# A shared 64 KB SBUF region for the PEER query weights, and twenty expert-table copies moved behind the last mixer block, in a streaming encoder step on one core

## The chip, the cores and the metric

One core of one Trainium2 chip. The metric is the device time of one execution in microseconds (us). The core's engines are named as the profile names them: PE (TensorE matmuls), PEld (its weight loads), DVE (VectorE), ACT (ScalarE), POOL (GpSimd) and SP (SyncE, which here only issues DMAs). POOL issues DMAs too: they run on the profile's queue q0. SP's run on q1.

## The reference

One layer over 1024 prompt frames (8 blocks of 128) and 8 x 16 sample frames (one block of 128): two mixers, then a PEER expert layer.

```python
h = rmsnorm(x, norm_mix)
qa, ka, va, qb, kb, vb, rg, ga, gb = project(h, w_in, b_gate)      # (1024, 5888)
oa = windowed attention(qa, ka, va)      # window 128, ALiBi, sinks
ob = retention(qb, kb, vb)               # per chunk, a state carried along
x += (sigmoid(ga) * (oa @ w_branch_a) + sigmoid(gb) * (ob @ w_branch_b)) @ w_out
h = rmsnorm(x, norm_ffn)
q = h @ w_q                              # (1024, 8 heads * 256)
s1, s2 = q1 @ sub_k1.T, q2 @ sub_k2.T    # 128 keys a side
idx, gate = best 16 of the 16 x 16 sums of the best 16 on each side, per head
u = expert_u[idx]; v = expert_v[idx]     # 128 rows of 1024 for each token
x += sum_k gate * gelu(h . u_k) * v_k
y = rmsnorm(x, norm_final)
```

Everything is float32. The outputs are y for both streams, the new key and value windows and the retention states.

## The kernel before

The 9 blocks of 128 tokens are block 0 (sample) and blocks 1 to 8 (prompt). The program is six `nc.Block` stages, one after another. At the end of each, the engines meet.

- **Stage A** (0 to 180 us): input projections of blocks 0 and 1.
- **Stage B** (to 346 us): the mixer of block 0.
- **Stage E** (to 458 us): the mixer of block 1. `prompt_buffers` and `score_buffers` give its tiles, among them the branch weights `wa` (16 KB a partition) and `wb` (32 KB), `wo` (32 KB), `zqk` (the part of z with queries and keys) and `alibi`. `pe_branches` multiplies by `wa` and `wb` and signals `ya`. `pe_output` then multiplies by `wo`. `store_rows` stores x and h2 when `x1` and `h2` are signalled.
- **Stage S** (to 1165 us): the expert search and experts of block 0, the search and the first 48 expert places of block 1, and the input projections of blocks 2 to 8 (line 1238). SP loads H, then with `load_search` the sub keys and all of `peer_w_q` (8 DMAs of 1 MB into `wq_s`), then the projections' inputs `xg` and the first two weight tiles `w`. PE waits for the query weights and runs `pe_keys` for two blocks, then the projections. POOL waits for the weights and for both tiles `w`, copies table parts, then gathers expert rows into `ring_s`.
- **Stage P** (to 1794 us): the mixers of blocks 2 to 8, one pass of a loop for each block; from pass 3 on a pass also ends the block before it (its branches, output, x and h2 stores). Between a block's steps `dve_point` puts expert groups of block 1: POOL gathers three rows of `peer_u` into `ru` (`pool_dots`) and three rows of `peer_v` into `rv` (`pool_values`), and DVE makes three dots (line 1472) and three accumulations (line 1489). Four such pairs of groups lie in a block, in a fixed order on DVE. The last, of dots, stands just ahead of `dve_residual` (line 446). After block 8 comes the stage's **tail**: block 8's own output, the last `rv` groups, and the query projection and search of block 2. For that, SP streams `peer_w_q` in 8 chunks of 1 MB through three buffers (`load_chunk`, line 1520). `qT`, the turned queries, lies over the first chunk buffer.
- **Last stage** (to the end): experts of blocks 2 to 8, 128 gathers for each block. One gather (line 2012) reads 8 KB per token, a row of u beside its row of v, from the interleaved table `uv_d` (128 MB, 128 parts). `load_search` loads `peer_w_q` once more (8 MB) on SP.

**The table.** `uv_d` is written by copies from DRAM to DRAM, one part being two DMAs of 512 KB. POOL issues parts 0 to 87 in stages A, B, E and S, at most two parts in flight (`pool_table`). SP issues parts 88 to 127 in stage P, eight in each of the passes 3 to 7 (`rest_of_table`, lines 244 and 245): two after the next block's `zqk` load, two when `prob` is signalled, two after the gates' load, two when the retention output `ro` is signalled. The first gather of the last stage waits for all of them.

**Order on SP's queue in the tail:** chunks 3 to 7, each when its buffer is free; then a wait for `x1` of block 8, the x store, a wait for `h2`, the h2 store, and the output of block 1.

## Time and profile before

| | us |
|---|---|
| median of 3 runs (4168.81, 4177.75, 4183.3) | 4177.75 |
| the profiled execution | 4131.7 |
| its span, first to last instruction | 4129.9 |

| engine | busy us | share of the span |
|---|---|---|
| PE | 3298.1 | 80% |
| PEld | 1643.4 | 40% |
| DVE | 2455.5 | 59% |
| ACT | 1088.2 | 26% |
| POOL | 1769.1 | 43% |

Read the DMA row first: the mean busy share of the 16 DMA engines in 40 slices of 103 us. Then come tables of stretches ("windows"), with each engine's busy time, PE's granted clock, the DMA share and the GB/s moved. A copy from DRAM to DRAM counts its bytes once.

### The profile page before, as it was taken

The page shows a single profiled execution, that of the slowest core. Times are in us where ns is not written, and L with a number is a line of the kernel's source. Part 1 is how long each engine was busy: PE and PEld are TensorE (multiplying, and loading weights), DVE is VectorE, ACT ScalarE, POOL GpSimd, SP SyncE. Part 2 cuts the span into 40 slices and gives each one's busy share as a digit, 9 for nine tenths or more (in the row PEclk, how much of TensorE's full clock was granted, in tenths as well). Part 3 has the DMA queues.
Part 4 walks back from the last instruction along what each step waited for, and adds up shares of the span by engine and source line. Part 5 has one row for each costly group of instructions (what it writes and reads, how often), then busy time and mean ns, then how long its engine had stood idle before and what let it go on. Part 6 is the DMA issues. An engine that isn't in the chain of part 4 may idle for free.

```text
span 4129.9 us, 32128 instructions
## 1 busy us (share of the span) xinstructions
PE 3298.1 (80%) x8957; PEld 1643.4 (40%) x8957; DVE 2455.5 (59%) x4977; ACT 1088.2 (26%) x2932; POOL 1769.1 (43%) x1588
## 2 busy tenths in 40 slices
PE   8775589999928878749779779878878977977776
PEld 5453256666524444324224323323323423422222
DVE  0122168998857677544864764674684585485454
ACT  2102011111113233213333333333333333323322
POOL 1020137787723333114444454444444444445554
PEclk9876799999958888969999999999999999999999
DMA  9898899999999998469999999999999999999998
GB/s 352 297 290 310 321 304 413 411 407 414 412 360 341 344 354 300 160 269 420 421 421 418 415 420 399 421 414 409 420 409 409 419 417 403 422 406 422 422 422 353
DMA packets 303586, 1563.05 MB, mean 378 GB/s; under 512 B 31280, under 2 KB 59184, under 8 KB 179888
## 3 DMA queue, kind: packets, MB, share of 16 engines
q0 software_dynamic: 228096, 1300.34, 78.7%
q1 hardware_dynamic: 60736, 239.86, 15.0%
q10 hardware_dynamic: 14592, 21.10, 1.4%
q8 instruction: 51, 0.84, 0.1%
q14 instruction: 111, 0.91, 0.1%
HBM read 1517.54 MB, written 179.04 MB: 411 GB/s over the span
## 4 chain that ended last, share of the span: by engine, by line
DMA 26%; PE 18%; issue 7%; DVE 4%; ACT 1%; POOL 1%; POOLq 0%; ACTq 0%; DVEq 0%
DMA ring<-uv_d,IXD_p 26%; PE ps L1807 14%; PE ps L1779 3%; DVE ring L1906 2%; ACT dg L1850 1%; DVE BV_p L979 1%; POOL ring L2012 1%; ACT GE_p L1844 0%; DVE BP_p L984 0%; DVE CA_p L989 0%; DVE VV_p L1332 0%; DVE CA_p L1397 0%; DVE DOT_p L1906 0%; DVE ACC L1887 0%; PE ps L1796 0%
## 5 line engine op out<-in xcount | busy, mean ns | idle before, releaser
L1807 PE MATMUL ps<-ring,dg 128*128 128x512 f32 x3584 | 1704.6, 614 | 474.3 <-ACT dg L1850 449.9
L2012 POOL DMA_INDIRECT ring<-uv_d,IXD_p x896 | 1082.3, 1208 | 1318.1 <-PE ps L1807 1068.0
L1906 DVE CUSTOM_DVE_ANT_0 ring<-ring,H 128x1024 f32<-128x1024 f32 x896 | 1094.2, 1223 | 907.3 <-DMA ring<-uv_d,IXD_p 886.6
L1807 PEld LDWEIGHTS ps<-ring,dg 128*128 128x128 f32 x3584 | 664.0, 194 | 1432.8 <-ACT dg L1850 714.3
L1238 PE MATMUL ps<-w,xg 128*128 128x368 f32 x1792 | 554.3, 472 | 2.0 <-ACT SC_s L936 2.0
L1844 ACT ACTIVATE GE_p<-DOT_p 128x2 f32<-128x2 f32 x448 | 91.1, 203 | 1502.6 <-DVE DOT_p L1906 1502.6
L1238 PEld LDWEIGHTS ps<-w,xg 128*128 128x128 f32 x1792 | 340.4, 190 | 215.5 <-ACT SC_s L936 2.2
L1850 ACT ACTIVATE dg<-gdi,GE_p 128x128 f32<-128x128 f32 x896 | 310.6, 393 | 46.6 <-ACT GE_p L1844 1.2
L1838 ACT ACTIVATE gdi<-ident,GD_p 128x128 f32<-128x128 f32 x896 | 303.1, 386 | 26.3 <-issue 19.9
L145 POOL DMA_DIRECT2D uv_d<-in_peer_u x88 | 45.6, 518 | 504.7 <-DMA uv_d<-in_peer_v 270.3
L1779 PE MATMUL ps<-wq,hT_p 128*128 128x512 f32 x384 | 197.9, 597 | 0.0
L1508 POOL DMA_INDIRECT rv<-in_peer_v,IXD x80 | 88.4, 1105 | 231.6 <-DVE AC L1489 215.2
L969 POOL DMA_INDIRECT ring_s<-in_peer_v,IXD_s x128 | 158.2, 1236 | 44.9 <-issue 38.4
L1101 DVE CUSTOM_DVE_ANT_0 ring_s<-ring_s,H_s 128x1024 f32<-128x1024 f32 x128 | 152.1, 1223 | 41.6 <-DMA ring_s<-in_peer_u,IXD_s 40.5
L969 POOL DMA_INDIRECT ring_s<-in_peer_u,IXD_s x128 | 152.6, 1192 | 47.3 <-issue 40.2
L226 PE MATMUL ps<-w,xg 128*128 128x368 f32 x512 | 161.4, 479 | 13.9 <-DMA w<-in_w_in 13.9
L1112 DVE SCALAR_TENSOR_TENSOR ACC_s<-ring_s,WG_s,ACC_s 128x1024 f32<-128x1024 f32 x126 | 157.1, 1290 | 13.3 <-DMA ring_s<-in_peer_v,IXD_s 12.9
L1267 ACT ACTIVATE zo<-ps,rstd 128x368 f32<-128x368 f32 x112 | 61.8, 566 | 373.4 <-PE ps L1238 371.9
L1516 POOL DMA_INDIRECT ru<-in_peer_u,IXD x80 | 82.1, 1027 | 151.7 <-DVE DOT L1472 117.1
L1472 DVE CUSTOM_DVE_ANT_0 ru<-ru,H 128x1024 f32<-128x1024 f32 x80 | 96.0, 1222 | 60.0 <-DMA ru<-in_peer_u,IXD 59.9
L226 PEld LDWEIGHTS ps<-w,xg 128*128 128x128 f32 x512 | 98.6, 193 | 76.0 <-issue 16.3
L1489 DVE SCALAR_TENSOR_TENSOR AC<-rv,WG,AC 128x1024 f32<-128x1024 f32 x80 | 102.7, 1284 | 40.8 <-DMA rv<-in_peer_v,IXD 36.1
(415 smaller groups left out, 2901.7 us busy)
## 6 DMA issues: line engine op xcount, KB each, us to landing
uv_d<-in_peer_u POOLq DMA_DIRECT2D x88, 512.0 KB, 5.4
uv_d<-in_peer_v POOLq DMA_DIRECT2D x88, 512.0 KB, 6.6
w<-in_w_in SPq DMA_DIRECT2D x8, 2944.0 KB, 15.1
w<-in_w_in SPq DMA_DIRECT2D x16, 1472.0 KB, 9.8
z_d<-zo ACTq DMA_DIRECT2D x16, 1288.0 KB, 18.8
uv_d<-in_peer_u SPq DMA_DIRECT2D x40, 512.0 KB, 9.6
uv_d<-in_peer_v SPq DMA_DIRECT2D x40, 512.0 KB, 11.3
ring<-uv_d,IXD_p POOLq DMA_INDIRECT x896, 11.2
```

Of the source, the lines that this page charges most:

```text
L226: mm = T.matmul(ps[:, m % AB, 0:WC], xg0[:, k, b * P:(b + 1) * P], w0[:, p % 2, n % 2, k, :], start=(k == 0), stop=(k == KT - 1))
L969: gather = g.indirect_dma_start(ring[:, n % RING, :], None, t["peer_u"] if kind == "u" else t["peer_v"], bass.IndirectOffsetOnAxis(ap=inde ...
L1101: V.tensor_tensor_reduce(out=row, in0=row, in1=H2[:], scale=1.0, scalar=0.0, op0=ALU.mult, op1=ALU.add, accum_out=DOT[:, k:k + 1]).then_in ...
L1112: V.scalar_tensor_tensor(ACC[:, k % 2], row, WG[:, k:k + 1], ACC[:, k % 2], ALU.mult, ALU.add).then_inc(d["freed"], 1)
L1238: mm = T.matmul(ps[:, n % AB, 0:WC], xg[:, k, b * P:(b + 1) * P], w[:, tile % 2, k, :], start=(k == 0), stop=(k == KT - 1))
L1489: V.scalar_tensor_tensor(AC1[:], row, WG1[:, k:k + 1], AC1[:], ALU.mult, ALU.add).then_inc(d["accz"], 1)
L1779: mm = T.matmul(bank(2 + n), hT[:, k, :], wq[:, k, n * 512:(n + 1) * 512], start=(k == 0), stop=(k == KT - 1))
L1807: mm = T.matmul(bank(6 + n), dg[:, k % DR, :], ring[:, k % RS, D + n * 512:D + (n + 1) * 512], start=(k == 0), stop=(k == NK - 1))
L1838: S.activation(gdi[:, k % GR, :], ident[:], ACT.Copy, scale=GD[:, k:k + 1]).then_inc(e["gdi"], 1)
L1850: S.activation(dg[:, k % DR, :], gdi[:, k % GR, :], ACT.Copy, scale=GE[:, k:k + 1]).then_inc(e["diag"], 1)
L1906: V.tensor_tensor_reduce(out=row, in0=row, in1=H2[:], scale=1.0, scalar=0.0, op0=ALU.mult, op1=ALU.add, accum_out=DOT[:, k:k + 1]).then_in ...
L2012: g.indirect_dma_start(ring[:, n % RS, :], None, uv_d, bass.IndirectOffsetOnAxis(ap=IXD[:, n:n + 1], axis=0)).then_inc(s_ring[n % RS], 16)
```

## The change

1. A region `rows64` of 64 KB a partition lives over stages E to the last. In stages E and P it holds `wa`, `wb`, `zqk` and `alibi` (and in P two of the three chunk buffers, over `zqk` and `alibi`). In stage S it holds the query weights `wq` and then the gather ring. In the last stage it holds `wq`.
2. In stage E, `load_queries` loads the 8 MB of query weights on SP's queue as soon as `ya` of block 1 is signalled, ahead of `store_rows`. Stage S no longer loads them.
3. In stage P, the passes 3 to 7 issue four table parts each in place of eight: two after the `zqk` load and two after the gates' load. SP's waits for `prob` and `ro` at that place go. The other 20 parts (108 to 127) are issued behind chunk 7 in the tail, with no wait of their own.
4. Chunks 6 and 7 stay where they land, as the last quarter of `wq`. For that `qT` moves from the first chunk buffer to `bg`. The other six chunks (6 MB) are loaded again in the tail when `ya` of block 8 is signalled, behind the 20 parts and ahead of the x store. The last stage loads no query weights.
5. `DOT1`, `GE1` and `WG1` shrink, and some tiles get other addresses.

```diff
-TABLE_A, TABLE_BS, TABLE_E, TABLE_S = 24, 46, 62, 88
+TABLE_A, TABLE_BS, TABLE_E, TABLE_S, TABLE_P = 24, 46, 62, 88, 108
...
+        def shared_rows():
+
+            return (rows64[:, 0:4 * D].rearrange("p (k n) -> p k n", k=4), rows64[:, 4 * D:FREE].rearrange("p (k n) -> p k n", k=KT),
+                    rows64[:, FREE:FREE + VB], rows64[:, FREE + VB:FREE + VB + HA * 2 * P].rearrange("p (h n) -> p h n", h=HA))
...
+        def load_queries(sp, blk, chunks):
+
+            sp.wait_ge(s["ya"], blk + 1)
+            for k in range(chunks):
+                sp.dma_start(wq[:, k], t["peer_w_q"][k * P:(k + 1) * P, :]).then_inc(s_cw, 16)
...
+        rows64 = sb(ctx, "rows64", [P, KT * PH * 256])
+        wq = rows64[:].rearrange("p (k n) -> p k n", k=KT)
+        FREE = 12 * D
...
                     load_branches(sp)
+                    load_queries(sp, 1, KT)
                     store_rows(sp, 1)
...
-        def load_search(sp):
+        def load_keys_tables(sp):
 
             sp.dma_start(kt[:, 0], t["sub_k1t"]).then_inc(s_cw, 16)
             sp.dma_start(kt[:, 1], t["sub_k2t"]).then_inc(s_cw, 16)
-            for k in range(KT):
-                sp.dma_start(wq[:, k], t["peer_w_q"][k * P:(k + 1) * P, :]).then_inc(s_cw, 16)
...
-            ring = sb(m, "ring_s", [P, RING, D])
+            ring = rows64[:].rearrange("p (r n) -> p r n", r=RING)
...
-            wqc = sb(b_, "wq_n", [P, 2, PH * 256])
+            wqc = rows64[:, FREE:].rearrange("p (j n) -> p j n", j=2)
...
-            qT = wqc[:, 0].rearrange("p (k n) -> p k n", n=P)
+            qT = bg[:].rearrange("p (k n) -> p k n", n=P)
...
-                        part = TABLE_S + 8 * (blk - 3)
+                        part = TABLE_S + 4 * (blk - 3)
                         if blk > 2:
-                            rest_of_table(sp, part, part + 2)
-                            sp.wait_ge(s["prob"], blk + 1)
-                            rest_of_table(sp, part + 2, part + 4)
+                            rest_of_table(sp, part, min(part + 2, TABLE_P))
...
-                            rest_of_table(sp, part + 4, part + 6)
-                            sp.wait_ge(s["ro"], blk + 1)
-                            rest_of_table(sp, part + 6, part + 8)
+                            rest_of_table(sp, part + 2, min(part + 4, TABLE_P))
...
                         load_chunk(sp, k)
+                    rest_of_table(sp, TABLE_P, NEXP // P)
+                    load_queries(sp, NB - 1, KT - 2)
                     sp.wait_ge(s["x1"], NB)
...
-            wq = sb(m, "wq", [P, KT, PH * 256])
...
-                            pe.wait_ge(s_cw, CW + 16 * (KT + 2))
+                            pe.wait_ge(s_cw, CW + 16 * KT)
...
-                    load_search(sp)
+                    load_keys_tables(sp)
```

## Rows read from the trace of the kernel before

**Rows 1.** The page: DMA busy share in tenths over 40 slices.

```profile
DMA  9898899999999998469999999999999999999998
```

**Rows 2.** Stretches: us, busy of PE, PEld, DVE, ACT, POOL, clock, DMA share, GB/s.

```profile
1250.00:1610.00 360.00, 290.92 (x993) 171.86 (x993) 255.89 (x403) 118.39 (x218) 128.74 (x118) 0.85 0.93 343
...
1725.00:1785.00 60.00, 33.41 (x84) 15.48 (x82) 56.88 (x212) 4.16 (x5) 0.00 (x0) 0.77 0.00 0
...
1860.00:2120.00 260.00, 218.59 (x523) 93.17 (x522) 177.21 (x420) 85.73 (x269) 123.19 (x104) 0.99 1.01 421
```

**Rows 3.** DMA issues, 1800 to 4100 us: queue, count, KB, us to landing.

```profile
wq<-in_peer_w_q SPq DMA_DIRECT2D x1, 1024.0 KB, 41.6
```

**Rows 4.** SP's timeline, first DMA of stage S: start, duration, line, tile, count.

```profile
458.45 0.34 SPq L1195 DMA_DIRECT2D H_s<-h_d  x1
```

**Rows 5.** DVE's timeline around `ya` in stage E.

```profile
423.79 1.22 DVE L438 TENSOR_TENSOR gates_e<-gates_e,ps 128x1024 f32<-128x1024 f32 x1 [24.37 <-PE ps L327]
```

**Rows 6.** PE's timeline: first instruction of stage S, in brackets its wait.

```profile
484.21 1.97 PE L907 MATMUL ps<-ident,H_s 128*128 128x128 f32 x8 [36.98 <-DMA wq_s<-in_peer_w_q]
```

**Rows 7.** POOL's timeline: table parts in stages E and S.

```profile
392.60 0.52 POOL L145 DMA_DIRECT2D uv_d<-in_peer_u  x1 [89.01 <-DMA wo_e<-in_w_out]
...
416.53 0.52 POOL L145 DMA_DIRECT2D uv_d<-in_peer_u  x1 [1.38 <-DMA uv_d<-in_peer_v]
...
423.83 0.52 POOL L145 DMA_DIRECT2D uv_d<-in_peer_u  x1 [1.49 <-DMA uv_d<-in_peer_v]
...
501.78 0.52 POOL L145 DMA_DIRECT2D uv_d<-in_peer_u  x1 [54.62 <-DMA w<-in_w_in]
```

**Rows 8.** SP's timeline, stage P: x stores of passes 4, 5, 7 and 8.

```profile
1381.96 0.34 SPq L1632 DMA_DIRECT2D x_d<-X_p  x1
...
1456.59 0.34 SPq L1632 DMA_DIRECT2D x_d<-X_p  x1
...
1603.61 0.34 SPq L1632 DMA_DIRECT2D x_d<-X_p  x1
...
1671.84 0.34 SPq L1632 DMA_DIRECT2D x_d<-X_p  x1
```

**Rows 9.** DVE's timeline, end of pass 5: first, last of six waiting rows; residual.

```profile
1441.02 1.28 DVE L1489 SCALAR_TENSOR_TENSOR AC<-rv,WG,AC 128x1024 f32<-128x1024 f32 x1 [1.55 <-DMA rv<-in_peer_v,IXD]
...
1454.19 1.23 DVE L1472 CUSTOM_DVE_ANT_0 ru<-ru,H 128x1024 f32<-128x1024 f32 x1 [1.23 <-DMA ru<-in_peer_u,IXD]
...
1455.35 1.22 DVE L446 TENSOR_TENSOR X_p<-X_p,ps 128x1024 f32<-128x1024 f32 x1
```

**Rows 10.** PE's timeline in pass 5: the output product.

```profile
1434.85 13.90 PE L340 MATMUL ps<-wo_p,yT_p 128*128 128x512 f32 x32
```

**Rows 11.** DVE's waits from 1603.6 to 1671.84 us (pass 8).

```profile
DVE X_p L446 <- PE ps L340: 5.3, 1, 5.3
```

**Rows 12.** DMA, 1250 to 1600 us: queues (packets, MB, share); gathers' median to landing.

```profile
q0 software_dynamic: 16437, 59.89, 46.4%
q1 hardware_dynamic: 14695, 60.31, 46.1%
...
rv<-in_peer_v,IXD POOLq DMA_INDIRECT x58, 8.7
```

**Rows 13.** SP's timeline in the tail: chunks 6 and 7, then the x store.

```profile
1691.38 3.76 SPq L1520 DMA_DIRECT2D wq_n<-in_peer_w_q  x2
...
1785.44 0.34 SPq L1646 DMA_DIRECT2D x_d<-X_p  x1
```

**Rows 14.** POOL's timeline in the tail: the last gather.

```profile
1703.80 0.94 POOL L1508 DMA_INDIRECT rv<-in_peer_v,IXD  x1 [0.30 <-issue]
```

**Rows 15.** DVE's timeline in the tail: last accumulation, start of the search.

```profile
1709.07 1.28 DVE L1489 SCALAR_TENSOR_TENSOR AC<-rv,WG,AC 128x1024 f32<-128x1024 f32 x1 [1.16 <-DMA rv<-in_peer_v,IXD]
...
1725.66 3.44 DVE L1332 MAX8 VV_n<-Pr_p 128x8 f32<-128x128 f32 x16 [9.84 <-ACT Pr_p L1580]
```

**Rows 16.** PE's timeline in the tail: branch product B of block 8.

```profile
1726.09 13.90 PE L1563 MATMUL ps<-wb_p,yT_p 128*128 128x512 f32 x32
```

More of the change, by code:

```diff
@@ L238, in trunk_kernel @@
         s_vstep, s_qbd, s_tab = sem("b_dve_step"), sem("b_qbd"), sem("b_prompt_tables")
-        s_uvs = sem("uv_table_rest")
+        s_uvs, s_cw = sem("uv_table_rest"), sem("c_weights")
         def rest_of_table(sp, lo, hi):
-            for part in range(lo, min(hi, NEXP // P)):
+            for part in range(lo, hi):
                 sp.dma_start(uv_d[part * P:(part + 1) * P, 0:D], rows(t["peer_u"], part)).then_inc(s_uvs, 16)
@@ L809, in trunk_kernel @@
         with ExitStack() as b_:
-            (zv, gates, X, Pr, atm, oaT, yn, yT, bg, gf, wa, wb, wo, qdT,
+            (zv, gates, X, Pr, atm, oaT, yn, yT, bg, gf, wo, qdT,
              outd, kdec, sink, mx, ngm, es, rs, stats, mv, sdv, sm2) = prompt_buffers(b_, "_e")
-            zqk, alibi, intra, into, qaT, qbT, kbT = score_buffers(b_, "_e")
+            intra, into, qaT, qbT, kbT = score_buffers(b_, "_e")
+            wa, wb, zqk, alibi = shared_rows()
             alibi_c = sb(b_, "alibi_c", [P, HA, P])
@@ L1432, in trunk_kernel @@
         with ExitStack() as b_:
-            (zv, gates, X, Pr, atm, oaT, yn, yT, bg, gf, wa, wb, wo, qdT,
+            (zv, gates, X, Pr, atm, oaT, yn, yT, bg, gf, wo, qdT,
              outd, kdec, sink, mx, ngm, es, rs, stats, mv, sdv, sm2) = prompt_buffers(b_, "_p")
@@ L1438, in trunk_kernel @@
             H21 = sb(b_, "H21", [P, D])
-            DOT1, GE1, WG1 = [sb(b_, n, [P, NK]) for n in ("DOT1", "GE1", "WG1")]
+            DOT1, GE1, WG1 = [sb(b_, n, [P, w]) for n, w in (("DOT1", REST), ("GE1", REST), ("WG1", SET))]
             m41 = sb(b_, "m41", [P, 4])
             with ExitStack() as scored:
-                zqk, alibi, intra, into, qaT, qbT, kbT = score_buffers(scored, "_p")
+                intra, into, qaT, qbT, kbT = score_buffers(scored, "_p")
+            wa, wb, zqk, alibi = shared_rows()
             hT = sb(b_, "hT_n", [P, KT, P])
-            wqc = sb(b_, "wq_n", [P, 2, PH * 256])
+            wqc = rows64[:, FREE:].rearrange("p (j n) -> p j n", j=2)
             kt = sb(b_, "kt_n", [P, 2, NKEY])
             nf1 = sb(b_, "nf_n", [P, D])
+            sb(b_, "score_rest", [P, 2 * P])
             with ExitStack() as dotted:
@@ L1488, in dve_expert_values @@
                         v.wait_ge(d["accz"], BASE_V + k)
-                    V.scalar_tensor_tensor(AC1[:], row, WG1[:, k:k + 1], AC1[:], ALU.mult, ALU.add).then_inc(d["accz"], 1)
+                    V.scalar_tensor_tensor(AC1[:], row, WG1[:, k % SET:k % SET + 1], AC1[:], ALU.mult, ALU.add).then_inc(d["accz"], 1)
             def dve_point(v, blk, j):
```

11 lines of the change are left out of this document (5 added, 6 removed).

## The prediction

> **What bounds the kernel now.** I read the page's DMA row first [rows 1]: the 16 DMA engines are busy 90% or more in most of the 40 slices. The exceptions lie around slices 17 and 18, the tail of stage P. Then I read the table of stretches [rows 2]. In the last stage the DMA engines are full (share 1.01, 421 GB/s) while PE is busy 219 of 260 us. That stage lasts as long as its bytes take. In the mixers the share is 0.93 at 343 GB/s. From 1725 to 1785 us it is 0.00 while DVE searches for 57 of 60 us. So one place has idle DMA engines, and the stages around it are bound, or nearly bound, by DMA. A byte counts for its full time in the last stage, partly in the mixers, and not at all in the tail's hole. Timelines, waits and DMA issues then give each part its place.
>
> **Part 1, the last stage loses its query load.** 8 DMAs of 1 MB are 8.4 MB. The one of them that lies in the listed stretch took 41.6 us to land [rows 3], since it shares full engines with the gathers. At 421 GB/s [rows 2] 8.4 MB are 19.9 us of all engines. PE, DVE and ACT have slack there, so nothing else comes last: **-20 us**. Bounds: -21, if the loads also slow the first gathers; -5, if much of their time lay in the fill of the eight ring buffers, where the first results wait anyway. I take the upper end, since the share is already 1.01 in a stretch that begins 66 us into the stage.
>
> The Trainium skill ("DMA: Bandwidth & Descriptors", section "Where 436 GB/s comes from") says that the HBM side, about 358 GB/s for a core, binds transfers between HBM and SBUF. By it this load would be worth 23 us, an estimate. The trace of this stage does not agree: it moves 421 GB/s [rows 2], and the measured rate decides.
>
> **Part 2, the load goes into stage E.** Before, H is loaded at 458.45 [rows 4] and PE's first work of stage S starts at 484.21, released by the query weights [rows 6]. After, SP issues the load when `ya` comes at 423.8, where DVE's wait for PE ends [rows 5]. What moves the same engines then: the 8.4 MB, the x and h2 stores (1.0 MB) and the rest of POOL's 16 parts of this stage. They start at 392.60, and two take 423.83 - 416.53 = 7.3 us [rows 7]. So 31.2 us are 8.5 parts, and some seven (7.3 MB) are left at 423.8. Together 16.7 MB at 343 to 421 GB/s [rows 2] take 40 to 49 us and end at 464 to 473. The x and h2 stores are queued behind the load on q1, and the stage waits for both. So stage E ends 6 to 14 us later than at 458. In return PE waits only for H and the small key tables, some 5 us into stage S: a first instruction at 469 to 478 against 484.2. POOL waits for both tiles `w`: 7.3 MB on q1, 18 to 21 us into the stage, 482 to 494 against 501.8 [rows 7]. From there PE's keys, the search and the projections follow as before, and PE is the later of the two. **-9 us**, bounds -15 and -3.
>
> **Part 3, the mixers lose four parts in each of five passes.** A pass takes 1456.59 - 1381.96 = 74.6 us, while pass 8, which has no parts, takes 1671.84 - 1603.61 = 68.2 us [rows 8]. At a pass's end DVE waits for gathers ahead of six instructions, 8.4 us in sum, and then adds the residual at 1455.35 [rows 9]. PE's output product for it ends at 1434.85 + 13.90 = 1448.75 [rows 10], so it has been done for 6.6 us. That is the most that faster gathers can give. Beyond it PE comes last, as in pass 8, where DVE waits 5.3 us for that product [rows 11]. The two parts at `ro` are issued among these gathers. At 343/0.93 = 369 GB/s [rows 2], 2.1 MB take 5.7 us of all engines. I take 5 us a pass. The two parts at `prob` land while DVE waits for PE's branch product in mid-pass, and I cost them at nothing. Their cover is that wait. SP's two removed waits hold only table parts behind them. 5 passes x 5 = **-25 us**, bounds 5 x 6.6 = -33 and 5 x 2 = -10. The lower bound is for the parts that stay, behind the gates' load, taking the freed share.
>
> **Part 4, the tail gets 20 parts and six loads.** SP is free for them at 1695.1 [rows 13], and chunks 6 and 7 go ahead of them on q1. 21.0 MB are 57 us at 369 GB/s, or 73 us at POOL's pace of 7.3 us for two [rows 2, 7]. So they end at 1756 to 1772. The six loads (6.3 MB, 15 us at 421) are issued at `ya`, 1726.1 + 13.9 = 1740 [rows 16], and land by 1771 to 1787. The x store comes at 1785.4 [rows 13]. It fits, with 14 us to spare or none, and the stores come later themselves by the next term. What is queued behind the new DMAs is that x store, the h2 store and the output of block 1. If they were late by 5 us, so would be the stage.
>
> The copies meet the last `rv` gathers. The last is issued at 1703.80 [rows 14], and DVE uses its row at 1709.07 [rows 15]: 5.3 us. In the mixers, with q1 as busy as q0 (60.31 and 59.89 MB), the median to landing is 8.7 us [rows 12]. DVE adds these rows up in order. ACT's square waits for the sum, the copies of the queries stand behind the square on ACT, and DVE's search at 1725.66 [rows 15] waits for these. So the 3.4 us go through to the stage's end: **+4 us**, bounds 0 and +12. Moving `qT` onto `bg`, the smaller tiles and the new addresses add no instruction: 0.
>
> **Sum.** -20 - 9 - 25 + 4 = -50 us. The profiled execution took 4131.7 us, so it becomes 4082. The median of the runs is 46 us higher. I take the difference as it is: 4177.75 - 50 = **4128 us**. The bounds add up to -69 and -6. All terms at one end together is unlikely.
>
> **Rivals.**
> - **The mixers have another bound.** If a pass is set by gathers whose time doesn't hang on the parts, or the two parts at the gates fill the freed share, the passes give about 1 us each: -30 in all, 4148 us. For it: two parts still lie just ahead of the critical gathers. Against it: pass 8 at 68.2 us.
> - **The last stage keeps its time**, because its fill hides the load. Then its term is -5, the sum -35, 4143 us. Against it: 421 GB/s throughout.
> - **Both together, or the change only moves bytes about:** -15 us or less, 4163 us or above.
> - **The tail starves the last gathers (slower).** 40 DMAs stand in q1 when POOL issues two small gathers on q0. If these get their turn only when q1 is empty, the last lands at about 1787 instead of 1709, the search starts 78 us later, and the sum is -54 + 78 = +24 us: 4202 us. It decides the sign once the two gathers lose over 54 us. Against it: in the mixers both queues moved the same bytes, with gathers landing in 8.7 us [rows 12]. There the code issues at most four copies at a time, which leaves it some chance. The Trainium skill ("DMA: Bandwidth & Descriptors", section "Queues, rings and completion order") says that each DMA engine takes packets of its queues in turn. By that rule, too, the gathers would keep a share, and this rival falls.
>
> **How the numbers follow.** Chances: my forecast 0.70, other bound in the mixers 0.12, last stage keeps its time 0.10, both 0.05, starvation 0.03. About 0.3% (12.5 us, so 4165 to 4190) is what a measurement of this kernel can tell from no change. The forecast and the first two rivals are faster by more than that: 0.92. "Both" counts as the same, 0.05, and starvation as slower, 0.03. The range runs from 4108 (the better bounds of all terms, -69) to 4153, which takes in the first two rivals.
>
> **What would show it.** Stage E: its h2 store lands 6 to 14 us later, PE's first work of stage S starts at 469 to 478. A pass takes 69 to 70 us, and the wait ahead of the residual is PE's. In the tail the zero share becomes a share near 1 until about 1770 (on the clock of before), and the last gather lands in 8 to 9 us. No query load stands in the last stage, which is 20 us shorter from its first gather. Wrong would be: passes above 72 us; the tail longer by over 12 us, by gathers or by late stores; the last stage shorter by less than 10 us.

## The result and the profile after

The median of the changed kernel is 4126.5 us (4113.8 to 4135.6), against 4180.5 us (4168.8 to 4183.6) for the kernel before, run beside it: **-54 us** between the medians. The ratio of runs taken together is 0.9884 with an interval of 0.9859 to 0.9910, which is -48 us (-38 to -59). The forecast was 4128 us and -50.

The two profiled executions don't show this gain. Before took 4131.7 us (span 4129.9), the changed kernel 4135.6 (span 4133.7), 4 us more. So the first job of reading is to find what hides 50 us. The page of the changed kernel, its DMA row (busy share in tenths over 40 slices, beside [rows 1]) and two rows of its groups (line, engine, operation, count | busy us, mean ns | idle before, releaser):

```profile
span 4133.7 us, 32125 instructions
...
DMA  9898999999998888889999999999999999999998
...
L1251 PE MATMUL ps<-w,xg 128*128 128x368 f32 x1792 | 581.0, 484 | 43.7 <-issue 41.7
```

The same group in the page of the kernel before:

```profile
L1238 PE MATMUL ps<-w,xg 128*128 128x368 f32 x1792 | 554.3, 472 | 2.0 <-ACT SC_s L936 2.0
```

These are the projection matmuls of stage S, which the diff doesn't touch. In the changed kernel's execution they stood still for 41.7 us for no cause that the profile shows ("issue"), and were slower by 27 us. In the page of before they did neither. The last section returns to this. To read the change itself, two executions without this stall have to be compared ("undisturbed" below). The experiments gave one: `after_third`, the changed kernel again, with a span of 4088.8 us. Table of stages (us; "to stage P" ends at SP's first DMA of stage P, "mixers" at the x store of pass 8, "tail" at the first DMA of the last stage; "stall" is the issue idle of the row above):

| execution | to stage P | mixers | tail | last stage | span | stall |
|---|---|---|---|---|---|---|
| before | 1165.7 | 506.2 | 122.3 | 2335.7 | 4129.9 | 0 |
| changed, `after` | 1204.5 | 483.8 | 127.3 | 2318.1 | 4133.7 | 41.7 |
| changed, `after_third` | 1162.8 | 482.3 | 123.5 | 2320.2 | 4088.8 | 0 |
| `after_third` - before | -2.9 | -23.9 | +1.2 | -15.5 | -41.1 | |
| forecast | -9 | -25 | +4 | -20 | -50 | |

The groups of rows of before, one by one.

**Mixers [rows 8 to 12].** SP's timeline in `after`, x stores of passes 4, 5 and 6 (start, duration, line, tile), and the stretch of the mixers (columns as in [rows 2]):

```profile
1343.32 0.35 SPq L1643 DMA_DIRECT2D x_d<-X_p  x1
...
1412.04 0.34 SPq L1643 DMA_DIRECT2D x_d<-X_p  x1
...
1480.96 0.34 SPq L1643 DMA_DIRECT2D x_d<-X_p  x1
```

```profile
1250.00:1610.00 360.00, 292.53 (x1002) 176.01 (x1003) 268.92 (x431) 119.78 (x218) 128.37 (x123) 0.83 0.86 311
```

A pass takes 68.7 and 68.9 us, where it took 74.6 [rows 8]. The DMA engines fell from 0.93 to 0.86 of the time. The end of that pass on DVE and PE (timelines of `after`):

```profile
1472.55 1.29 DVE L1504 SCALAR_TENSOR_TENSOR AC<-rv,WG,AC 128x1024 f32<-128x1024 f32 x1 [1.13 <-DMA rv<-in_peer_v,IXD]
1474.85 1.28 DVE L1504 SCALAR_TENSOR_TENSOR AC<-rv,WG,AC 128x1024 f32<-128x1024 f32 x1 [1.01 <-DMA rv<-in_peer_v,IXD]
...
1479.72 1.22 DVE L446 TENSOR_TENSOR X_p<-X_p,ps 128x1024 f32<-128x1024 f32 x1
```

```profile
1465.60 13.90 PE L340 MATMUL ps<-wo_p,yT_p 128*128 128x512 f32 x32
```

Two short waits for gathers are left of six. The residual starts at 1479.72, and PE's output product ends at 1465.60 + 13.90 = 1479.50. Before, that product had been done for 6.6 us [rows 9, 10]. Now it ends together with DVE's own dots. The forecast had said that the wait ahead of the residual would be PE's; DVE waits there for PE in one of the passes 4 to 7 (0.9 us), and in the other three it works right up to the residual.

**Tail [rows 13 to 16].** SP's timeline of `after`: the end of the copies, the six query loads, the stores, and the first DMA of the last stage. Then the last gather on POOL's timeline, and DVE's use of it:

```profile
1771.06 1.62 SPq L245 DMA_DIRECT2D uv_d<-in_peer_v  x1
1772.73 10.37 SPq L808 DMA_DIRECT2D rows<-in_peer_w_q  x6
1806.89 0.34 SPq L1659 DMA_DIRECT2D x_d<-X_p  x1
1811.10 0.34 SPq L1661 DMA_DIRECT2D h_d<-yT_p  x1
...
1815.59 0.34 SPq L1943 DMA_DIRECT2D H<-h_d  x1
```

```profile
1719.92 0.93 POOL L1523 DMA_INDIRECT rv<-in_peer_v,IXD  x1 [0.30 <-issue]
```

```profile
1731.20 1.28 DVE L1504 SCALAR_TENSOR_TENSOR AC<-rv,WG,AC 128x1024 f32<-128x1024 f32 x1 [1.89 <-DMA rv<-in_peer_v,IXD]
```

From the gather's issue to DVE's use of its row it is 11.3 us, against 5.3 before [rows 14, 15]. The stretches of the tail in `after` (pass 8's x store is at 1688.3, 16.4 us later than in [rows 8]):

```profile
1725.00:1750.00 25.00, 15.84 (x70) 10.53 (x69) 8.11 (x20) 8.56 (x10) 0.00 (x0) 0.86 1.02 312
1750.00:1775.00 25.00, 11.46 (x27) 4.75 (x25) 23.54 (x127) 0.00 (x0) 0.00 (x0) 0.78 1.03 327
...
1785.00:1795.00 10.00, 10.00 (x25) 4.42 (x24) 9.72 (x27) 0.31 (x1) 0.00 (x0) 1.00 1.01 402
1795.00:1807.00 12.00, 1.40 (x4) 0.33 (x2) 11.76 (x11) 0.10 (x1) 0.00 (x0) 0.78 0.49 206
```

The hole of 0.00 [rows 2] is filled. In a finer cut the share falls from 0.69 at 1800 to 0.05 at 1804, so the engines run empty at about 1803, 4 us before the x store is issued at 1806.89.

**Last stage [rows 2, 3].** No query load is issued in it. It still moves 417 GB/s at a share of 1.01, and it is 17.6 us shorter than before (15.5 in `after_third`, 18.0 in `after_again`).

**Stages E and S [rows 4 to 7].** SP's timeline and waits (us in total, times, longest) from stage E into S, POOL's last part of stage E, and PE's first work of stage S:

```profile
424.04 4.02 SPq L808 DMA_DIRECT2D rows<-in_peer_w_q  x8
448.84 0.34 SPq L299 DMA_DIRECT2D x_d<-X_e  x1
453.05 0.34 SPq L301 DMA_DIRECT2D h_d<-yT_e  x1
474.25 0.34 SPq L1208 DMA_DIRECT2D H_s<-h_d  x1
```

```profile
SPq L847 <- DMA h_d<-yT_e: 11.0, 1, 11.0
SPq L834 <- PEq L834: 9.5, 1, 9.5
```

```profile
467.16 0.52 POOL L146 DMA_DIRECT2D uv_d<-in_peer_v  x1
```

```profile
478.68 1.97 PE L921 MATMUL ps<-ident,H_s 128*128 128x128 f32 x8 [31.12 <-DMA kt_s<-in_sub_k2t]
```

Stage E ends 474.25 - 458.45 = 15.8 us later than before [rows 4], not 6 to 14. PE starts at 478.7 against 484.2 [rows 6], just outside the forecast's 469 to 478. But stage P does not begin 9 us earlier: 2.9 in the undisturbed pair. That is the part whose mechanism the forecast had wrong, and the experiments on it come third.

### The profile page after: what moved, and what is told of

It is laid out like the page before. It is cut to its first block, busy times and chain, and to the rows that moved or that the text cites. A ratio compares the mean times of both kernels' runs of the same rounds, so it can differ in the third digit from the quotient of the medians.

```text
span 4133.7 us, 32125 instructions
## 1 busy us (share of the span) xinstructions
PE 3319.9 (80%) x8957; PEld 1647.3 (40%) x8957; DVE 2453.0 (59%) x4977; ACT 1089.3 (26%) x2932; POOL 1761.3 (43%) x1588
## 4 chain that ended last, share of the span: by engine, by line
DMA 25%; PE 18%; issue 7%; DVE 4%; ACT 1%; POOL 1%; POOLq 0%; ACTq 0%; DVEq 0%
DMA ring<-uv_d,IXD_p 25%; PE ps L1819 15%; PE ps L1791 3%; DVE ring L1918 2%; ACT dg L1862 1%; POOL ring L2024 1%; DVE BV_p L993 1%; ACT GE_p L1856 0%; DVE BP_p L998 0%; DVE CA_p L1003 0%; DVE VV_p L1345 0%; PE ps L1808 0%; DVE CA_p L1410 0%; DVE DOT_p L1918 0%; DVE ACC L1899 0%
## 5 line engine op out<-in xcount | busy, mean ns | idle before, releaser
L1251 PE MATMUL ps<-w,xg 128*128 128x368 f32 x1792 | 581.0, 484 | 43.7 <-issue 41.7
L145 POOL DMA_DIRECT2D uv_d<-in_peer_u x88 | 45.6, 518 | 501.3 <-DMA uv_d<-in_peer_v 292.3
L1791 PE MATMUL ps<-rows,hT_p 128*128 128x512 f32 x384 | 196.5, 593 | 0.0
L983 POOL DMA_INDIRECT rows<-in_peer_u,IXD_s x128 | 154.5, 1207 | 54.6 <-issue 40.1
L983 POOL DMA_INDIRECT rows<-in_peer_v,IXD_s x128 | 151.4, 1183 | 53.5 <-issue 37.8
L226 PE MATMUL ps<-w,xg 128*128 128x368 f32 x512 | 161.3, 479 | 14.3 <-DMA w<-in_w_in 14.3
L1115 DVE CUSTOM_DVE_ANT_0 rows<-rows,H_s 128x1024 f32<-128x1024 f32 x128 | 151.3, 1219 | 35.3 <-DMA rows<-in_peer_u,IXD_s 24.1
L1126 DVE SCALAR_TENSOR_TENSOR ACC_s<-rows,WG_s,ACC_s 128x1024 f32<-128x1024 f32 x126 | 155.1, 1293 | 0.7 <-DVE ACC_s L1122 0.5
L226 PEld LDWEIGHTS ps<-w,xg 128*128 128x128 f32 x512 | 98.6, 193 | 76.4 <-issue 16.7
L1504 DVE SCALAR_TENSOR_TENSOR AC<-rv,WG,AC 128x1024 f32<-128x1024 f32 x80 | 102.7, 1284 | 41.1 <-DMA rv<-in_peer_v,IXD 36.0
```

The costliest lines, as they stand in the source:

```text
L226: mm = T.matmul(ps[:, m % AB, 0:WC], xg0[:, k, b * P:(b + 1) * P], w0[:, p % 2, n % 2, k, :], start=(k == 0), stop=(k == KT - 1))
L983: gather = g.indirect_dma_start(ring[:, n % RING, :], None, t["peer_u"] if kind == "u" else t["peer_v"], bass.IndirectOffsetOnAxis(ap=inde ...
L1115: V.tensor_tensor_reduce(out=row, in0=row, in1=H2[:], scale=1.0, scalar=0.0, op0=ALU.mult, op1=ALU.add, accum_out=DOT[:, k:k + 1]).then_in ...
L1126: V.scalar_tensor_tensor(ACC[:, k % 2], row, WG[:, k:k + 1], ACC[:, k % 2], ALU.mult, ALU.add).then_inc(d["freed"], 1)
L1251: mm = T.matmul(ps[:, n % AB, 0:WC], xg[:, k, b * P:(b + 1) * P], w[:, tile % 2, k, :], start=(k == 0), stop=(k == KT - 1))
L1504: V.scalar_tensor_tensor(AC1[:], row, WG1[:, k % SET:k % SET + 1], AC1[:], ALU.mult, ALU.add).then_inc(d["accz"], 1)
```

## The experiments

All ratios are to the kernel before, run in the same round on the same chip. Chips and hours differ: the median of the kernel before was 4154, 4171, 4133 and 4129 us in the four groups below. Unless said otherwise an edit is made to the changed kernel.

### Both kernels again

`after_again` and `after_third` are the changed kernel, `before_again` the kernel before, all without an edit.

> The changed kernel once more, beside the kernel before, as the reference for the three runs after it. The medians said -54 us, but the two profiled executions differ by +4 us (4131.7 and 4135.6): between 568 and 1191 us PE's projection matmuls stood still for 42 us in all with no releaser, which they did not in the trace of before. Theory 1 (the stall is a matter of the single execution and strikes either kernel): the ratio is again near 0.988, and this trace has a stall of another size, anywhere from 0 to 60 us. Theory 2 (the stall belongs to the changed kernel, and its gathers' ring in another place or the earlier load brings it): the stall is again near 42 us in stage S, and the ratio rests on something that the two traces don't show.

> The kernel before once more, for a second trace of it. All five traces with the shared region show PE's projection matmuls of stage S standing still for 20 to 49 us in all, with no releaser; the one trace of before shows 0. Theory 1 (a matter of the execution that strikes any of these kernels, and the first trace of before happened to be free of it): this trace shows such stalls too, with stage S above 715 us where the first trace has 707. It would explain why the runs of before that were not profiled lie 24 to 50 us above its trace. Theory 2 (the shared region or the earlier start of the stage brings the stalls): stage S is again 707 us with none.

> The changed kernel a third time, beside the three runs before it in this job. Stage S is expected between 700 and 760 us with PE's stalls, every other stage within 2 us of its first two traces: passes of 69 us, a tail of 126 to 128, a last stage of 2318.

Measured: `after_again` 4115.4 us, 0.9899 (0.9855 to 0.9942); `after_third` 4090.2 us, 0.9896 (0.9879 to 0.9912); `before_again` 4161.4 us, 0.9973 (0.9946 to 1.0000). So three measurements of the change agree at 0.988 to 0.990, -42 to -48 us, and the narrowest says **-43**. The same kernel against itself can be 0.3% off in one round, and the forecast's bound for "no change" was well chosen. What the profiled executions show decides more. Groups of PE in `before_again` and `after_third`:

```profile
L1238 PE MATMUL ps<-w,xg 128*128 128x368 f32 x1792 | 576.7, 481 | 60.2 <-issue 58.1 <-ACT SC_s L936 2.0
```

```profile
span 4088.8 us, 32125 instructions
...
L1251 PE MATMUL ps<-w,xg 128*128 128x368 f32 x1792 | 554.6, 472 | 2.1 <-ACT SC_s L950 2.0
```

The kernel before has the stall too: 58.1 us in one execution, none in another, and the spans are 4178.6 and 4129.9. The changed kernel has 41.7 and 0, and the spans are 4133.7 and 4088.8. Within each kernel the difference in span lies in stage S: 756.5 - 707.2 = 49.3 of 48.7 us before, 730.2 - 688.2 = 42.0 of 44.9 after. So the stall strikes both kernels and is no effect of the change. `before_again` and `after`, which both have it, differ by -44.9 us, and `before` and `after_third`, which both don't, by -41.1. The first two profiled executions looked alike because one had it and the other had not.

### Part 3, the mixers: the parts back at their places

`parts_back` gives the mixers 8 parts a pass again, at their four old places, and the tail none.

```diff
-part = TABLE_S + 4 * (blk - 3)
+part = TABLE_S + 8 * (blk - 3)
...
-    rest_of_table(sp, part, min(part + 2, TABLE_P))
+    rest_of_table(sp, part, min(part + 2, NEXP // P))
+    sp.wait_ge(s["prob"], blk + 1)
+    rest_of_table(sp, part + 2, min(part + 4, NEXP // P))
...
-rest_of_table(sp, part + 2, min(part + 4, TABLE_P))
+rest_of_table(sp, part + 4, min(part + 6, NEXP // P))
+sp.wait_ge(s["ro"], blk + 1)
+rest_of_table(sp, part + 6, min(part + 8, NEXP // P))
...
-rest_of_table(sp, TABLE_P, NEXP // P)
```

> The changed kernel with its 20 table parts put back into the passes 3 to 7, eight in each with both waits; the shared region and all loads of query weights stay as changed. Theory 1 (the mixers gave 22 us and the tail took 5 by the parts): passes of 74 us in place of 69, the tail from the x store of pass 8 to the first DMA of the last stage 122 to 123 us in place of 127, and 17 to 21 us longer in all, a ratio to before of 0.992 to 0.993. Rival (the passes are shorter for another reason, as the lighter use of the chunk buffers): passes of 69 to 70 us, and a time 5 us below the changed kernel's.

Measured: 4133.9 us, 0.9953 (0.9926 to 0.9980), against 0.9899 for the changed kernel in the same group. In the trace the mixers take 505.9 us, as before (506.2), and the tail 122.0 (122.3). SP's timeline of `parts_back`, x stores of passes 5 and 6:

```profile
1419.09 0.34 SPq L1647 DMA_DIRECT2D x_d<-X_p  x1
...
1493.05 0.34 SPq L1647 DMA_DIRECT2D x_d<-X_p  x1
```

74.0 us a pass. The parts alone make the 22 to 24 us of the mixers; the shared region and the moved loads, which this kernel keeps, make none of them. (The ratio lies above the expected 0.992 to 0.993. Stalls in stage S differ from run to run and blur it, 49.2 us in the profiled one; the marks of mixers and tail hold none of them.)

`prob_parts` asks the question that the forecast had answered with "nothing": what do parts in mid-pass cost? It gives back two parts a pass, at `prob` alone, so 30 stay in the mixers and 10 go to the tail.

```diff
-TABLE_A, TABLE_BS, TABLE_E, TABLE_S, TABLE_P = 24, 46, 62, 88, 108
+TABLE_A, TABLE_BS, TABLE_E, TABLE_S, TABLE_P = 24, 46, 62, 88, 118
...
-part = TABLE_S + 4 * (blk - 3)
+part = TABLE_S + 6 * (blk - 3)
...
     rest_of_table(sp, part, min(part + 2, TABLE_P))
+    sp.wait_ge(s["prob"], blk + 1)
+    rest_of_table(sp, part + 2, min(part + 4, TABLE_P))
...
-rest_of_table(sp, part + 2, min(part + 4, TABLE_P))
+rest_of_table(sp, part + 4, min(part + 6, TABLE_P))
```

> The changed kernel with 10 of the 20 moved parts put back, two a pass, where SP waited for the probabilities, in mid-pass; the tail keeps 10. It tests the step of my prediction that costs these mid-pass parts at nothing, their cover being DVE's wait for the branch product of PE. Theory: passes stay at 69 us, and the tail is 122 to 126 us. Rival (what counts is the number of parts a pass, wherever they stand): passes of 71 to 72 us, half way back to 74.

Measured: 4089.5 us, 0.9892 (0.9875 to 0.9908); the changed kernel in the same group 4090.2. SP's timeline, x stores of passes 4, 5 and 6:

```profile
1302.36 0.35 SPq L1645 DMA_DIRECT2D x_d<-X_p  x1
...
1371.33 0.34 SPq L1645 DMA_DIRECT2D x_d<-X_p  x1
...
1442.10 0.34 SPq L1645 DMA_DIRECT2D x_d<-X_p  x1
```

The passes are 69.0, 70.8, 68.2, 69.4 and 68.5 us, the mixers 483.6. Two parts in mid-pass cost nothing that can be seen. DVE still waits 3.0 and 7.1 us for PE's branch product in the passes to 1442 and 1510, so the cover was not used up. That the place of a copy counts, and not only the number a pass, shows in where a pass got shorter. It has two legs on SP's timeline, from the x store to the gates' load and from there to the next x store (passes 4 to 7):

| execution | parts a pass (of these at `prob`, at `ro`) | x store to gates' load | gates' load to x store |
|---|---|---|---|
| before | 8 (2, 2) | 44.9 to 46.2 | 27.8 to 29.0 |
| `parts_back` | 8 (2, 2) | 44.9 to 46.0 | 27.9 to 29.0 |
| `prob_parts` | 6 (2, 0) | 45.4 to 45.6 | 22.7 to 25.3 |
| `after` | 4 (0, 0) | 45.2 to 46.5 | 23.0 to 23.5 |

The first leg is the same with and without the parts at `prob`. The second, which has the last gathers and the parts at `ro`, is some 5 us longer where those parts stand. No run has parts at `ro` and none at `prob`, so what two parts at `ro` cost without the two at `prob` is read from these legs and was not tried by itself.

### Part 1, the last stage: the load back in it

```diff
-load_queries(sp, NB - 1, KT - 2)
...
 load_keys_tables(sp)
+for k in range(KT - 2):
+    sp.dma_start(wq[:, k], t["peer_w_q"][k * P:(k + 1) * P, :]).then_inc(s_cw, 16)
```

> The changed kernel with the load of six query chunks (6.3 MB) taken out of the tail and put at the start of the last stage, on the same queue ahead of X1. Theory 1 (the last stage lasts as long as its bytes): 6.3 MB at 421 GB/s are 15 us, so 15 us longer than the changed kernel in the last stage, the tail 0 to 1 us shorter. Rival (the fill of the ring hides the load): 5 us longer or less.

Measured: 4129.3 us, 0.9943 (0.9917 to 0.9969), against 0.9899 in the same group. The last stage takes 2330.8 us against 2317.7 of `after_again`: +13.1 us for 6.3 MB. Its rate, in the stretch of [rows 2]:

```profile
1860.00:2120.00 260.00, 211.78 (x503) 89.00 (x502) 177.08 (x418) 85.11 (x267) 128.43 (x106) 0.99 1.01 421
```

At 421 GB/s 6.3 MB are 15.0 us, and 13.1 came. So the stage is bound by bytes, and some 2 us of the load cost nothing. The only room that the traces show is in the stage's first 10 us, where the share is 0.85 (306 GB/s) in `after_again` and 0.93 (343 GB/s) with the load; from then on it is 1.01 or more in both. That room holds some 1 us of the load. The same share of the whole load, 8.4 MB, gives 13.1 / 15.0 x 19.9 = 17.4 us, and 15.5 to 18.0 were measured. (Chunks 6 and 7, which the changed kernel keeps from the tail's own search, were not put back.)

### Part 2, stages E and S

`load_in_s` and `load_in_s_2` are one kernel: the query load stands at its old place behind the keys, and all else is as changed.

```diff
-load_queries(sp, 1, KT)
...
 load_keys_tables(sp)
+for k in range(KT):
+    sp.dma_start(wq[:, k], t["peer_w_q"][k * P:(k + 1) * P, :]).then_inc(s_cw, 16)
```

> The changed kernel without the query load in stage E: the 8 MB are loaded at the start of stage S, into the same shared region, in the order of the kernel before. My prediction says 9 us longer than the changed kernel. The two traces say less: stage S began at 474.2 in place of 458.5, and PE's projections at 568.5 in place of 572.9, so 4 to 5 us longer. Rival (the load beside POOL's copies is worth nothing, since the engines are full either way): within 2 us of the changed kernel.

> The kernel without the query load in stage E a second time, to size that part by itself. In the traces so far POOL's first gather of stage S comes 166 to 172 us after stage E's branch product in the nine kernels with the early load, 172 in this one, and 174 and 177 in the two traces of before. Theory (stage S is paced by POOL's copies and gathers, so PE's earlier start is worth nothing and the early load only the 3 to 4 us by which the gathers start sooner): first gather again 172 to 175 us after the product, ratio to before 0.990 to 0.992 where the changed kernel had 0.990, and stage S to the end 3 to 4 us later where PE doesn't stall. Rival (my predicted 9 us): first gather at 177 or later, ratio 0.992 or above.

Measured: 4122.3 us, 0.9925 (0.9893 to 0.9956), and 4096.5 us, 0.9922 (0.9908 to 0.9935). Against 0.9896 the step is worth 0.0026 x 4130 = 11 us by these ratios, but the intervals overlap. The traces give less, and show where. Times in us after `ya` comes, in undisturbed executions:

| | stage S starts | PE's first work | projections start | POOL's first gather | stage P starts |
|---|---|---|---|---|---|
| before | 34.7 | 60.4 | 149.1 | 173.7 | 741.9 |
| `load_in_s_2` | 35.0 | 60.0 | 149.0 | 177.7 | 746.0 |
| changed (`after_third`) | 48.6 | 52.9 | 141.5 | 168.8 | 736.8 |
| `prob_parts`, both stages as changed | 51.4 | 56.4 | 145.4 | 172.1 | 740.0 |
| `pool_less` (below) | 36.0 | 40.2 | 130.0 | 169.8 | 738.6 |

PE gains 7.5 us and the projections 7.6 in `after_third`, 4.0 and 3.7 in `prob_parts`. The end of the stage gains 5.1 and 1.9 against before. With the load put back it loses 4.1 against before, which nothing in the edit explains, so marks that far along can be off by some 4 us. The first gather is the steadier mark, since it lies ahead of the stall and every execution has it: it comes at 165.6 to 172.1 in the ten executions with the early load, mean 169.2, and at 172.0 to 177.7 in the four without it, mean 175.1. So the early load is worth some 6 us there. The last expectation had called 177 or later, with a ratio of 0.992 or above, the sign of the predicted 9 us; `load_in_s_2` gave both, but `load_in_s` gave 172.0. Between 2 and 11 us the size stays open.

**Why does stage E end so late?** The forecast said that the x and h2 stores are queued behind the load. They are: SP waits 11.0 us for the h2 store in `after`, until 464.4, which is 6.8 us later than before. `stores_act` gives them a queue of their own, by letting ACT issue them.

```diff
-store_rows(sp, 1)
...
+act.wait_ge(s["x1"], 2)
+act.dma_start(rows(x1_d, 1), X[:]).then_inc(s["x1st"], 16)
 act_norm2(act, 1)
+act.wait_ge(s["h2"], 2)
+act.dma_start(rows(h2_d, 1), HO[:]).then_inc(s["h2st"], 16)
```

> The changed kernel with stage E's x and h2 stores issued on ACT's queue, so that they don't stand behind the 8 MB of query weights on SP's. Theory (stage E ends 16 us later only because both stores queue behind that load): stage E ends 34 to 40 us after its branch product, as in the kernel before, in place of 48 to 50; stage S then waits for the rest of the load, and PE's projections start 0 to 8 us earlier. Rival (the engines are full, and the order of the queues only moves the wait): projections within 2 us of 142 us after the branch product, as now.

Measured: 4131.8 us, 0.9880 (0.9827 to 0.9933); the execution profiled had a stall of 56.4 us. ACT issued the h2 store at 450.98, and stage S still started 49.6 us after `ya`. SP's waits in it:

```profile
SPq L834 <- PEq L834: 12.5, 1, 12.5
```

The stores had landed, and SP stood 12.5 us at the end of the stage, which all engines have to reach. The rival holds: the stores are not what ends stage E. In `after` SP stopped waiting for them at about 465 and then stood 9.5 us. PE, DVE and ACT had ended by 453. Only POOL was left: it issued its last part at 467.16, 20.5 us later than before (446.65). Beside the query load it issued one part each 7.4 us (440.84, 448.29 and 455.74), where it issued two in 7.3 before [rows 7]: the DMA engines are full there, with a share of 1.01 from 424 to 465 us against 0.83 from 424 to 458 before. They moved bytes until about 472, so whether the stage waits for POOL's last issue or also for that part's landing is not shown.

**If POOL is last, fewer parts for it should help.** `pool_less` moves four parts from stage E to stage S.

```diff
-TABLE_A, TABLE_BS, TABLE_E, TABLE_S, TABLE_P = 24, 46, 62, 88, 108
+TABLE_A, TABLE_BS, TABLE_E, TABLE_S, TABLE_P = 24, 46, 58, 88, 108
```

> The changed kernel with TABLE_E at 58 in place of 62: POOL issues 12 parts in stage E and 30 in stage S, in place of 16 and 26. Theory (stage E now ends when POOL has issued its last part, slowed by the query load beside it, and no longer with the stores): POOL's last issue comes some 15 us earlier, stage E ends 38 to 43 us after its branch product in place of 48 to 50, and the projections start 5 to 10 us earlier, at 132 to 137 us after that product in place of 141 to 144. Rival (something else in the stage's end is slow, as the query load itself): stage E ends at 47 us or later after the product, and stage S has 4 parts more to copy before its gathers.

Measured: 4094.7 us, 0.9906 (0.9890 to 0.9923), so not faster than the changed kernel (0.9896). The timelines of PE and POOL in `pool_less`:

```profile
465.46 1.97 PE L921 MATMUL ps<-ident,H_s 128*128 128x128 f32 x8 [17.60 <-DMA kt_s<-in_sub_k2t]
```

```profile
441.38 0.52 POOL L146 DMA_DIRECT2D uv_d<-in_peer_v  x1
...
594.02 0.52 POOL L146 DMA_DIRECT2D uv_d<-in_peer_v  x1
595.00 1.00 POOL L983 DMA_INDIRECT rows<-in_peer_u,IXD_s  x1 [0.46 <-issue]
```

And POOL in `after_third`:

```profile
593.85 0.52 POOL L146 DMA_DIRECT2D uv_d<-in_peer_v  x1
594.82 1.00 POOL L983 DMA_INDIRECT rows<-in_peer_u,IXD_s  x1 [0.46 <-issue]
```

The cause of the late end was right: POOL's last part is issued at 441.4, stage E ends 36.0 us after `ya` instead of 48.6 (now with the h2 store: SP waits 7.0 us for it and then only 0.2), and PE and the projections are 11.5 to 13 us earlier. But POOL's last copy of stage S stands at 594.0 against 593.9, its gathers begin right behind it, and stage P starts at 1163.8 against 1162.8. The 12 us were given to an engine that is not last: PE's last projection matmul ends 37 us before stage P in `pool_less`, 41 us in `after_third` and 38 us before the change. What ends the stage is DVE with POOL's last gathered rows. So stage S is paced by what POOL must copy and then gather, that is by the bytes of both stages together, and a part moved from E to S only moves its bytes ahead of the same gathers.

### Part 4, the tail

`parts_late` keeps the copies from the last `rv` gathers: SP waits until the sum is complete.

```diff
+sp.wait_ge(d["accz"], BASE_V + REST)
 rest_of_table(sp, TABLE_P, NEXP // P)
 load_queries(sp, NB - 1, KT - 2)
```

> The changed kernel with one wait more on SP: the 20 parts of the tail are issued only when DVE has added up the last gathered row. Theory (the parts slow the last two gathers, and the chain through ACT's square hands that to the search): the last row is used 5 us after its gather's issue as in the kernel before, not 11, and the tail is 122 to 124 us in place of 126 to 127. Rival (the parts start about 12 us later and end behind the search, so the x store waits behind them): the tail is 127 us or longer.

Measured: 4125.0 us, 0.9889 (0.9835 to 0.9944). SP's timeline: 

```profile
1768.24 9.32 SPq L808 DMA_DIRECT2D rows<-in_peer_w_q  x6
1789.14 0.34 SPq L1660 DMA_DIRECT2D x_d<-X_p  x1
1793.35 0.34 SPq L1662 DMA_DIRECT2D h_d<-yT_p  x1
...
1804.33 0.34 SPq L1944 DMA_DIRECT2D H<-h_d  x1
```

The x store is issued 113.2 us after pass 8's, as before (113.6), against 118.6 in `after`. In `parts_late` the last row is used 5.2 us after its gather's issue, as in before (5.3), and the search starts 53.5 us after pass 8's x store (before 53.8, `after` 58.9). So the 5 us are the late gathers, shown by their removal. But the stage gains nothing (tail 128.4). Counted from pass 8's x store, the query loads are issued 8 us later (92.3 against 84.5) and the x store 5 us earlier, and there were only 4 us to spare. The stores queue behind the loads, and from the h2 store to the last stage's first DMA it is 11.0 us instead of 4.5. The rival of that run came true: the tail holds 20 parts and six loads, but not behind this wait.

`best` puts the pieces together: 10 parts in mid-pass (free), 10 in the tail behind the wait (they fit), and stage E's cut of `pool_less`. The rest of its edit is that of `prob_parts` and of `parts_late`.

```diff
-TABLE_A, TABLE_BS, TABLE_E, TABLE_S, TABLE_P = 24, 46, 62, 88, 108
+TABLE_A, TABLE_BS, TABLE_E, TABLE_S, TABLE_P = 24, 46, 58, 88, 118
...
```

> All that the runs so far point to, on the changed kernel: 12 parts in place of 16 in stage E, two parts in mid-pass as well as four, so that the tail has 10, and these 10 issued only when DVE has added up the last gathered row. If the three pieces hold, against the changed kernel: projections 5 to 8 us earlier, passes 69 us, tail 122 us in place of 126 to 128; 10 to 13 us in all, so a ratio to before of 0.986 to 0.989. If the mid-pass parts cost half of their bytes, 12 us of that go again, and it is no better than the changed kernel.

Measured: 4081.3 us, 0.9873 (0.9857 to 0.9889): the fastest of both kernels and all edits, 51 us below before and 9 below the changed kernel's median in that group. The two intervals overlap a little (0.9879 to 0.9912 for the latter), but the slowest of its four runs (4082.9) is faster than the fastest of the changed kernel's four (4088.0). The tail is 122.0 us, as before the change, with all of its work in it. The query loads are issued at 1709.7, as soon as `ya` comes and long before the x store:

```profile
1709.72 2.71 SPq L808 DMA_DIRECT2D rows<-in_peer_w_q  x6
...
1755.14 0.34 SPq L1662 DMA_DIRECT2D x_d<-X_p  x1
...
1763.85 0.34 SPq L1946 DMA_DIRECT2D H<-h_d  x1
```

Against `after_third` the tail is 1.5 us shorter. The rest of the 9 lies in the mixers (3.2) and the last stage (4.9, but 2.4 against `after_again`), where no piece of the edit was meant to save anything, and may be scatter. The early end of stage E gave nothing, as in `pool_less`: stage P starts at 1162.8 in both.

## Why the prediction was right, and where it was off

**The time.** 4128 forecast, 4126.5 measured. Part of that is luck. The sum was -50, and three measurements give -48, -42 and -43 by their ratios, the undisturbed pair -41.1. The true step is nearer to -43, and the forecast was some 7 us too good. The medians, 54 us apart, lie further apart than the step. A second choice was lucky too: "The median of the runs is 46 us higher. I take the difference as it is". It was not known what the 46 us were. The profiled execution of before had no stall in stage S, and one of 4180 us (`before_again`) had 58.1 us of it, so most of the 46 us were probably such stalls; runs that were not profiled can't show it. On the chips of the last two groups the medians of before were 4133 and 4129, at its own profiled time.

**Mixers, -25: right, mechanism and size.** -22.4 and -23.9 were measured, and the experiment that puts the parts back returns them. A pass takes 69 us (forecast 69 to 70), PE's output product is done 0.0 to 1.5 us before the residual instead of 6.6, and the parts in mid-pass cost nothing, as assumed. The rival "The mixers have another bound" falls. One sign was put too strongly: DVE seldom waits for PE there, the two arrive together.

**Last stage, -20: right in mechanism, 2 to 4.5 us too large.** The failed step is "I take the upper end". The share of 1.01 was read in a stretch that begins 66 us into the stage; the load stood ahead of that, and in the first 10 us the share is 0.85. Of 15.0 us put back, 13.1 came. The rival "The last stage keeps its time" falls.

**Stages E and S, -9: inside its bounds at best, with the wrong mechanism.** 1.9 and 5.1 us came at the stage's end, some 6 at POOL's first gather, 11 by ratios whose intervals overlap; the bounds were 3 and 15. The sum of bytes held: 16.7 MB were to end at 464 to 473, and the engines ran empty at about 472. Two steps failed. First, "The x and h2 stores are queued behind the load on q1, and the stage waits for both. So stage E ends 6 to 14 us later". The h2 store did land 6.8 us later, but the stage ended 15.8 us later, since the stores were not last. The forecast had counted POOL's seven remaining parts in the bytes, yet followed only the queue of the stores; POOL issues a part only when an earlier one has landed, and the stage can't end before POOL has issued its last. Second, "PE is the later of the two". PE did gain 7.5 us, and in `pool_less` 20 us against before, but those 12.7 us more moved the stage's end by nothing. POOL's copies, then its gathers, set the pace. The forecast's own estimate for POOL (8 to 20 us earlier at the wait for `w`) came out smaller: `w` released it 73.3 us after `ya` against 78.0, 4.7 us earlier, and 6.9 in `after_third`.

**Tail, +4: right in mechanism, of uncertain size.** +5.0, +3.4 and +1.2 were measured for the changed kernel, and +7.3 and +7.4 in `load_in_s` and `stores_act`, whose tail has the same code. The gathers lost more than the 3.4 us forecast: 9.5 to 11.6 us from issue to use, where the forecast took 8.7. "It fits, with 14 us to spare or none" was right, near the lower end: some 4 us were left in `after`. The rival of starvation falls: the last gather of `after` was used at 1731 while the copies and loads kept the engines busy until 1803. But its premise didn't come either. SP had issued only 11 of the 40 copies when POOL issued that gather, and 17 when its row was used, so a queue of 40 was never tried. The Trainium skill ("DMA: Bandwidth & Descriptors", section "Queues, rings and completion order") says that an engine takes packets of its queues in turn, and the trace agrees in so far as both gathers landed long before SP's queue was empty.

**The rate.** By the 358 GB/s of the Trainium skill ("DMA: Bandwidth & Descriptors", section "Where 436 GB/s comes from") the load would be worth 23 us in the last stage, an estimate. The runs speak against that: the stage moved 414 to 421 GB/s, and 6.3 MB back in it cost 13.1 us.

## What to carry to other kernels

A byte has the price of its place: two table parts cost some 5 us at the end of a pass, among the gathers that DVE waits for, and nothing in mid-pass under a wait for PE. Before you give an engine an earlier start, find who sets the end of the stage; here PE got up to 20 us and the stage some 5, since POOL's copies and gathers paced it. And before you compare two profiled executions, look for stretches that the diff doesn't touch: they should be equal, and where they aren't, that difference comes off first.

## What the runs showed of the hardware

**PE can stand still with nothing to wait for.** In stage S of seven of the fourteen executions profiled, of either kernel and of the edits, the projection matmuls had 35 to 58 us of idle time without a releaser; one had 19.5 and the others none or 10 to 12, which ACT had caused. How it looks in `after` (PE's timeline, and the stretch around it):

```profile
686.58 0.77 PE L1251 MATMUL ps<-w,xg 128*128 128x368 f32 x1 [1.35 <-issue]
688.68 0.77 PE L1251 MATMUL ps<-w,xg 128*128 128x368 f32 x1 [1.33 <-issue]
```

```profile
675.00:700.00 25.00, 9.56 (x14) 3.94 (x14) 21.83 (x44) 1.20 (x3) 16.58 (x16) 0.50 1.02 409
```

And in the kernel before, in `before_again`:

```profile
683.55 0.77 PE L1238 MATMUL ps<-w,xg 128*128 128x368 f32 x1 [2.03 <-issue]
```

```profile
640.00:700.00 60.00, 19.83 (x34) 8.11 (x33) 46.89 (x70) 1.19 (x3) 40.12 (x42) 0.57 1.03 410
```

One matmul starts every 2.1 or 2.8 us, multiples of 0.70 us. The granted clock is 0.50 in the first of these stretches, the lower of the two levels (1.2 GHz), where PE was busy 9.56 of 25 us, and the DMA engines are full at 409 to 410 GB/s. It came in groups: in the first two groups of experiments every profiled execution had it, in the last two none. What starts it stays open. The profile doesn't tell whether loads of instructions were late (their queue q8 moved no packet from 640 to 700 us in `before_again` and one in `before` and in `after`), and nothing was tried against it.

**The stall reaches the stage's end through ACT.** Without a stall PE ends 37 to 41 us before stage P starts, so the stall doesn't add up one for one: 19.5 us of it (`load_in_last`) went with a stage S of 691.1 us against 688.2 in `after_third`, 41.7 and 58.1 us with 42.0 and 49.3 us more. In ACT's program the gelus of block 0's experts (`GE_s`), which DVE needs, stand at fixed places among the copies of PE's projection results, so they are late when PE is. DVE's waits in `after`:

```profile
DVE WG_s L1104 <- ACT GE_s L959: 45.6, 3, 28.6
```

The same wait is 34 to 65 us in the seven executions with a large stall, 13.0 in `load_in_last`, and does not occur in the six without one. POOL's first gathers for block 1, which wait for DVE's indices, then wait 30 to 52 us instead of 5 to 12.

**Copies alone don't fill the engines' rate.** In the tail the copies within DRAM moved 312 and 327 GB/s at a share of 1.02 and 1.03, where loads and gathers move 402 to 421. At 320 GB/s the tail's 21 MB are 66 us rather than the 57 that the forecast took from the mixers' 369 GB/s as its better end.

**Many copies in a row hold the engine that issues them.** In `after` SP issued its first copies of the tail one each 0.6 us, and from the twelfth on one each 1.8 us on the mean (52.5 us for the last 29), until 1772.7. That is 290 GB/s, worked out from 29 copies of 512 KB, and near what the DMA engines moved there. The six loads took 10.4 us to issue, where eight took 4.0 in stage E. They stood behind the copies in SP's program: `ya` came at 1761.5, and their issue began 11.3 us later; in `best`, with half the copies, it began with `ya`. What stands behind such a run of copies is late by their drain, not only by its own transfer.
